# A one-core encoder layer whose mixing stage is put in another order: forward transforms before the heads, spectral products between the heads' steps, the inverse in the last head

## The chip, the cores and the metric

The kernel runs on one core of one Trainium2 chip. The metric is the device time of one execution in microseconds; lower is better.

## What is computed

One layer of an encoder trunk on a sequence of 512 tokens of width 1024, all in float32:

```
x = x + 0.5 * swiglu(rmsnorm(x), w_gate, w_up, w_down)        # first half-step, d_ff 2816
p = rmsnorm(x) @ w_in           # -> q | k | v | x0 | x1 | v_hy, each 512 wide
a = differential attention      # 4 heads, two softmaxes per head (64 wide each), T5 bias:
                                #   attn = p[:, 0] - lam * p[:, 1]; out = rmsnorm(attn @ v)
y = hyena(x0, x1, v_hy)         # width-3 conv on each; v = v_hy * x1;
                                # v = irfft(rfft(v, 1024) * rfft(kern, 1024)) + v * bias;
                                # y = rmsnorm(v * x0) in 8 groups of 64
x = x + concat([a, y]) @ w_out
x = x + 0.5 * swiglu(rmsnorm(x), ...)                         # second half-step
out = rmsnorm(x)
```

The filter `kern` comes out of a small network with sines, times a decay.

## The kernel before, in words

Five engines run programs written out by hand, one block each (SyncE, GpSimd, ScalarE, VectorE, TensorE; SP, POOL, ACT, DVE and PE below), tied together by semaphores alone; no scheduler moves anything. Activations lie transposed in SBUF, 128 channels by 512 tokens to a block `k`.

**Weight tiles.** All dense products run in float32 split into two parts. A weight tile of 8 blocks of 128x128 is loaded by SP into one of four `raw` buffers (512 KB), ACT rounds it into `w_hi` (`split`, L447), DVE makes `w_lo = raw - w_hi` (`split`, L713), each into one of two halves, and PE runs 24 matmuls per tile, `w_hi*hi`, `w_hi*lo`, `w_lo*hi` for each of 8 blocks (`tile`, L1137 to L1139). A load waits for the split of the tile four before, a split for PE to have used the tile two before. Everything else is woven into this stream.

**Stages.** First half-step (44 gate and up tiles, 24 down tiles), mixing, second half-step, final norm. The mixing stage has 24 projection tiles (`project`, matmuls of 8 blocks of x with one 128-wide part of `w_in`) and 8 output tiles (`out_half`). The token norm is applied after the product: `sum_squares` (L1150) sums over channels with one 128x128 matmul of ones on 512 columns, ACT takes the root and DVE the reciprocal (L753) of all 512 columns in `rinv`.

**A head** before the change has 6 projections (q, k, v, x0, x1, v_hy of head and group h). Between them stand four blocks of `scores` (L1255 to L1257, 2 banks of 128x512 for one block of 128 queries). Their way on: DVE `logits` (scale and bias, L904, then the row's extreme, L909), ACT `exps` (L557), DVE `combine` (L914 to L919), which normalises both softmaxes and writes `attn`. `attend` (L1278, L1286) turns `attn` on PE, ACT copies it (L577), PE multiplies it by v. `attend(h)` comes in the next head, behind its second projection. The three hyena projections get their width-3 conv by ACT `tap` and DVE `taps` (L926, L927).

**After the last head** come, in this order on PE: the kernel's forward transform (`kernel_sums`, L1369), column sums of squares for the attention norm (`col_sums`, L1328), `attend(3)`, the spreading of the inverse norms over a bank (`spread`, L1356), the forward transform of the signal (`forward`, L1403), output tile 0, then `inverse(0)` (L1417), output tile 1, the rest of the inverse, output tile 2 around the hyena's column sums (L1332) and spreads, output tiles 3 to 7. The transforms are split by parity of tokens and by near and far half of the spectrum (f = 0, 1). The spectral product per f is 4 sums of even and odd parts (L1050 to L1057), 8 products (L1041), the real parts (L1077 to L1086) on DVE, and the imaginary parts on POOL (L413 to L430).

```
combine(near, prod[:, 4, :], prod[:, 5, :], ALU.add)        # POOL, L417
mult(prod[:, 0, :], near_a, near_p)                         # DVE, L1041
nc.vector.tensor_tensor(near_a, prod[:, 0, :], prod[:, 1, :], ALU.subtract)   # L1077
pe.wait_ge((spec_set, spec_q_set)[k], f + 1)                # PE, ahead of inverse(f)
```

## Time and profile before

| what | value |
| --- | --- |
| device time, median of 3 runs | 1061.95 us (1061.38 to 1062.06) |
| device time of the profiled execution | 1061.0 us |
| its span, first to last instruction | 1059.2 us |
| mean granted TensorE clock | 0.99 |
| PE, DVE, ACT, POOL busy | 98%, 54%, 32%, 6% |
| mixing stage on PE (first projection to last output tile) | 378.4 to 685.1 us |
| DMA | 96.69 MB, mean 91 GB/s |

The profiled execution took 1061.0 us on the clock that the runs are timed with, of which 1059.2 lie between its first and last instruction. A PE that is busy 98% of the span has a matmul in flight almost always; it does not say that the matmul ran at the full clock, which is told by the granted clock (1.00 is 2.4 GHz, 0.50 is 1.2 GHz). A fp32 matmul that is not split (`L1369`, `L1403`, `L1286` and others) appears as two records in the trace, a transpose and a split matmul as one.

### The profile page before, as it was taken

To read this page: it belongs to the slowest core of one execution; us is meant where nothing else is said; L and a number is where in the kernel's file an instruction comes from. 1 tells how busy PE (TensorE), PEld (TensorE's weight loads), DVE (VectorE), ACT (ScalarE), POOL (GpSimd) and SP (SyncE) were. 2 spreads that over 40 slices of the span, in tenths; PEclk is the share of its full clock that TensorE was granted. 3 is DMA by queue.
4 is the path that set the end of the run, shared out by engine and by line. 5 is a ranking of instruction groups with operands and counts; after the bars stand their busy time and mean duration, and the time that the engine had idled before them with its cause. 6 is when DMAs were issued, how large, how long until landed. Compare 5 with 4: busy or idle time off the path is not lost. (4 is left out here: it accounts for less than half of the span.)

```text
span 1059.2 us, 12002 instructions
## 1 busy us (share of the span) xinstructions
PE 1034.5 (98%) x4551; PEld 821.8 (78%) x4551; DVE 569.8 (54%) x722; ACT 335.2 (32%) x477; POOL 60.7 (6%) x57
## 2 busy tenths in 40 slices
PE   9999999999999999999999969999999999999996
PEld 8887888888777867777775558878888888888885
DVE  5545444454544458695876695764544444433332
ACT  6222222222222333444444203532222222222222
POOL 0000000000000010000000160300000000000000
PEclk9999999999999999999999989999999999999999
DMA  7743332333233361322211000323333333333322
GB/s 221 165 118 90 100 99 86 98 95 101 83 94 105 90 199 40 97 78 80 80 60 40 1 20 21 99 87 98 94 99 99 99 99 90 96 97 91 94 70 79
DMA packets 184460, 96.69 MB, mean 91 GB/s; under 512 B 14811, under 2 KB 181859, under 8 KB 184424
## 3 DMA queue, kind: packets, MB, share of 16 engines
q1 hardware_dynamic: 183160, 92.70, 30.2%
q0 software_dynamic: 352, 1.85, 0.6%
q10 hardware_dynamic: 912, 1.64, 0.5%
q8 instruction: 24, 0.39, 0.2%
q14 instruction: 12, 0.10, 0.0%
HBM read 94.07 MB, written 2.11 MB: 91 GB/s over the span
## 5 line engine op out<-in xcount | busy, mean ns | idle before, releaser
L1137 PE MATMUL bank<-x_hi,w_hi 128*128 128x512 f32 x880 | 347.0, 394 | 0.8 <-DVE x_lo L748 0.4
L1139 PE MATMUL bank<-x_hi,w_lo 128*128 128x512 f32 x880 | 342.6, 389 | 0.0
L1138 PE MATMUL bank<-x_lo,w_hi 128*128 128x512 f32 x880 | 342.6, 389 | 0.0
L713 DVE TENSOR_TENSOR w_lo<-raw,w_hi 128x1024 fp32r<-128x1024 f32 x168 | 203.6, 1212 | 220.9 <-ACT w_hi L447 216.5
L447 ACT CAST w_hi<-raw 128x1024 fp32r<-128x1024 f32 x168 | 172.3, 1026 | 167.4 <-PE bank L1139 131.8
L1137 PEld LDWEIGHTS bank<-x_hi,w_hi 128*128 128x128 f32 x880 | 165.2, 188 | 43.2 <-issue 7.0
L1139 PEld LDWEIGHTS bank<-x_hi,w_lo 128*128 128x128 f32 x880 | 165.2, 188 | 34.7
L1138 PEld LDWEIGHTS bank<-x_lo,w_hi 128*128 128x128 f32 x880 | 165.3, 188 | 34.6 <-issue 1.2
L1137 PE MATMUL bank<-h_hi,w_hi 128*128 128x512 f32 x352 | 137.3, 390 | 0.0
L1139 PE MATMUL bank<-h_hi,w_lo 128*128 128x512 f32 x352 | 137.0, 389 | 0.0
L1138 PE MATMUL bank<-h_lo,w_hi 128*128 128x512 f32 x352 | 136.9, 389 | 0.0
L492 ACT CAST h_hi<-bank 128x512 f32 (+1 forms) x44 | 25.8, 587 | 199.2 <-DVE bank L808 199.2
L1137 PEld LDWEIGHTS bank<-h_hi,w_hi 128*128 128x128 f32 x352 | 66.1, 188 | 15.9 <-DVE resid L728 1.6
L1139 PEld LDWEIGHTS bank<-h_hi,w_lo 128*128 128x128 f32 x352 | 66.1, 188 | 13.8
L1138 PEld LDWEIGHTS bank<-h_lo,w_hi 128*128 128x128 f32 x352 | 66.1, 188 | 13.7
L803 DVE TENSOR_TENSOR bank<-bank,rinv 128x512 f32<-128x512 f32 x44 | 30.8, 699 | 75.4 <-PE bank L1139 75.4
L387 POOL TENSOR_TENSOR ssq<-ssq,sq 128x512 f32<-128x512 f32 x24 | 32.3, 1348 | 655.0 <-ACT sq L454 654.7
L488 ACT ACTIVATE silu<-bank 128x512 f32<-128x512 f32 x44 | 26.3, 598 | 134.4 <-DVE bank L799 134.4
L799 DVE TENSOR_TENSOR bank<-bank,rinv 128x512 f32<-128x512 f32 x44 | 30.8, 699 | 41.3 <-PE bank L1139 41.3
L811 DVE TENSOR_TENSOR h_lo<-bank,h_hi 128x512 f32 (+1 forms) x44 | 30.5, 692 | 36.7 <-ACT h_hi L492 36.7
L454 ACT ACTIVATE sq<-resid 128x512 f32<-128x512 f32 x24 | 15.1, 630 | 76.3 <-DVE resid L728 65.1
L808 DVE TENSOR_TENSOR bank<-bank,silu 128x512 f32<-128x512 f32 x44 | 30.8, 700 | 4.5
(207 smaller groups left out, 783.3 us busy)
## 6 DMA issues: line engine op xcount, KB each, us to landing
raw<-in_ffn_w_gate SPq DMA_DIRECT2D x44, 512.0 KB, 3.8
raw<-in_ffn_w_up SPq DMA_DIRECT2D x44, 512.0 KB, 3.7
raw<-in_ffn_w_down SPq DMA_DIRECT2D x32, 512.0 KB, 3.5
raw<-in_w_in SPq DMA_DIRECT2D x24, 512.0 KB, 3.7
raw<-in_ffn_w_down SPq DMA_DIRECT2D x16, 384.0 KB, 3.0
raw<-in_w_out SPq DMA_DIRECT2D x8, 512.0 KB, 3.4
x_nat<-in_x SPq DMA_DIRECT2D x4, 512.0 KB, 7.1
out<-o_nat SPq DMA_DIRECT2D x8, 256.0 KB, 2.9
```

The source lines that it names most:

```text
L387: nc.gpsimd.tensor_tensor(ssq[:], ssq[:], sq[:, b, :], ALU.add).then_inc(ssq_added, 1)
L447: nc.scalar.copy(w_hi[:, half, 0:kb, :], raw[:, slot, 0:kb, :]).then_inc(w_hi_made, 1)
L488: nc.scalar.activation(silu[:, b, :], bank[b][:], ACT.Silu).then_inc(gate_act, 1)
L492: nc.scalar.copy(h_hi[:, number(b, 2, i), :], bank[2 + b][:]).then_inc(h_hi_made, 1)
L713: nc.vector.tensor_tensor(w_lo[:, half, 0:kb, :], raw[:, slot, 0:kb, :], w_hi[:, half, 0:kb, :].bitcast(F32), ALU.subtract).then_inc(w_spl ...
L799: nc.vector.tensor_tensor(bank[b][:], bank[b][:], rinv[:], ALU.mult).then_inc(gate_scaled, 1)
L803: nc.vector.tensor_tensor(bank[2 + b][:], bank[2 + b][:], rinv[:], ALU.mult).then_inc(up_scaled, 1)
L808: nc.vector.tensor_tensor(bank[2 + b][:], bank[2 + b][:], silu[:, b, :], ALU.mult).then_inc(h_made, 1)
L811: nc.vector.tensor_tensor(h_lo[:, at, :], bank[2 + b][:], h_hi[:, at, :].bitcast(F32), ALU.subtract).then_inc(h_split, 1)
L1137: nc.tensor.matmul(dst, w_hi[:, half, k, :], hi, start=first and k == 0, stop=False)
L1138: nc.tensor.matmul(dst, w_hi[:, half, k, :], lo, start=False, stop=False)
L1139: ins = nc.tensor.matmul(dst, w_lo[:, half, k, :], hi, start=False, stop=last and k == kb - 1)
```

## The change

- **Order of projections.** `SEQ` puts the 8 projections of x1 and v_hy ahead of the heads; a head then has 4 (q, k, v, x0), `project(n)` counts them 0 to 23.
- **Transforms.** The kernel's transform is done between projections 4 and 7, the signal's forward transform at the first head (`forward(0)` before it, `forward(1)` in it). The inverse, now by group of channels (`inverse(g)`), is in head 3.
- **Spectral products** are cut into pairs of DVE operations (`cosines`, `sines`, `cross_near`, `own_far`, `real` and so on) and put between the attention steps of heads 0 to 2. POOL has no part in them any more.
- **Logits** and row extreme are one instruction (`tensor_tensor_reduce`, two rows in the order below); the bias table is multiplied by 8 where it is made. `combine` no longer scales both softmaxes: `attn = p0 - (lam * s0 / s1) * p1`, the factor 1/s0 goes into the norm's statistics afterwards. One [128, 512] multiplication by a scalar (L916) a block goes.
- **attend**: its first two turns stand inside the head's last projection tile, 3 matmuls before its end, and the rest right behind it, in the same head.
- **Token norm**: four matmuls on one column each, root and reciprocal of [128, 4], then four 128x128 matmuls that spread it (`spread_tokens`) inside the next tile, and a copy. This is also so in the second half-step.
- **Room**: the kernel's spectra lie where `resid` was. `resid` (2 MB) is stored to DRAM by SP behind the load of projection tile 3 and brought back behind the load of output tile 1, once the inverse is done.
- **Output tiles**: the hyena's half first, then the attention's. The norm of the hyena part is done around the last projection, that of the attention part between output tiles.

```diff
+OUT_TILES = [(1, 0), (1, 1), (1, 2), (1, 3), (0, 0), (0, 1), (0, 2), (0, 3)]
+OUT_BANKS = [(0, 1), (2, 3), (4, 5), (6, 7)]
+SEQ = [(4, 0), (5, 0), (4, 1), (5, 1), (4, 2), (5, 2), (4, 3), (5, 3)]
+SEQ += [(m, h) for h in range(HEADS) for m in (0, 1, 2, 3)]
...
+FORWARD_BANKS = (4, 5, 6, 7)
+INV_BANKS = (4, 5, 4, 5)
+SPREAD_BANKS = (2, 3, 2, 3)
+ATT_BANKS = (6, 7, 6, 7)
...
+    for n, (m, g) in enumerate(SEQ):
+        load(w[:, :, m * D_ATT + g * P:m * D_ATT + (g + 1) * P], KD, N_MIX + n)
+        if n == 3:
+            sp.wait_ge(resid_set, KD)
+            sp.dma_start(resid_dram, resid[:]).then_inc(resid_saved, 16)
...
+        if n == 1:
+            sp.wait_ge(resid_saved, 16)
+            sp.wait_ge(long_sum, NG)
+            sp.dma_start(resid[:], resid_dram).then_inc(resid_back, 16)
...
-        pool.wait_ge(prod_set, 2 * f + 1)
-        if f == 0:
...
-        combine(near, prod[:, 4, :], prod[:, 5, :], ALU.add)
-        ins = combine(far, prod[:, 6, :], prod[:, 7, :], ALU.add)
-        ins.then_inc(prod_read, 1)
-        pool.wait_ge(prod_read, 2 * f + 1)
...
+        nc.scalar.activation(x_r[:, 4:8], bank[7][:, 0:NT], ACT.Sqrt, bias=eps[:], scale=1.0 / D).then_inc(root_made, 1)
...
+        nc.vector.reciprocal(x_r[:, 8:12], x_r[:, 4:8]).then_inc(tok_inv, 1)
+    def widen_rinv(s):
+        dve.wait_ge(tok_spread, s)
+        nc.vector.tensor_copy(rinv[:], bank[7][:]).then_inc(rinv_made, 1)
...
-            nc.vector.scalar_tensor_tensor(logit[:, c, :], bank[2 + c][:], -(DK ** -0.5), near,
-                                           ALU.mult, ALU.subtract).then_inc(logit_set, 1)
-        for c in range(2):
-            n = 2 * (NT * h + qb) + c
-            dve.wait_ge(logit_set, n + 1)
-            nc.vector.tensor_reduce(soft[:, c:c + 1], logit[:, c, :], AX.X, ALU.min).then_inc(max_set, 1)
+            nc.vector.tensor_tensor_reduce(logit[:, c, :], bank[2 + c][:], near, -(DK ** -0.5), LEAST,
+                                           ALU.add, ALU.min, stat[:, c:c + 1]).then_inc(logit_set, 1)
...
-        dve.wait_ge(prob_set, 2 * (NT * h + qb) + 2)
-        link(nc.vector.reciprocal(soft[:, 4:6], soft[:, 2:4]))
-        link(nc.vector.tensor_tensor(soft[:, 6:7], soft[:, 5:6], lam[:, 5:6], ALU.mult))
-        link(nc.vector.tensor_scalar(prob[:, 1, :], prob[:, 1, :], soft[:, 6:7], None, ALU.mult))
+        i = NT * h + qb
+        dve.wait_ge(prob_set, 2 * i + 2)
+        s0, s1 = (stat[:, 16 + 2 * i + c:17 + 2 * i + c] for c in range(2))
+        link(nc.vector.reciprocal(stat[:, 2:3], s1))
+        link(nc.vector.scalar_tensor_tensor(stat[:, 3:4], s0, lam[:, 5:6], stat[:, 2:3], ALU.mult, ALU.mult))
         if h and qb == 0:
             dve.wait_ge(attn_turned, NT * h)
-        nc.vector.scalar_tensor_tensor(attn[:, qb, :], prob[:, 0, :], soft[:, 4:5], prob[:, 1, :],
+        nc.vector.scalar_tensor_tensor(attn[:, qb, :], prob[:, 1, :], stat[:, 3:4], prob[:, 0, :],
                                        ALU.mult, ALU.add).then_inc(attn_set, 1)
-    def taps(h, m):
-        dst = x0c[:, h, :] if m == 0 else conv[:, m - 1, :]
-        dve.wait_ge(tap_set, 3 * h + m + 1)
...
+    def cross_near(f):
+        near_a, far_a, near_b, far_b = parts(f)
+        mult(t0, near_a, kern_q[:, f, :])
+        link(mult(t1, near_b, kern_p[:, f, :]))
...
+    minus_lambda()
+    logits(0, 0)
+    first_row()
+    combine(0, 0)
+    project(10)
+    split(8, N_MIX + 12)
+    cross_near(0)
+    cross_far(0)
+    cosines(1)
+    sines(1)
+    logits(0, 1)
+    own_near(0)
+    combine(0, 1)
+    project(11)
+    logits(0, 2)
+    split(8, N_MIX + 13)
+    taps(11)
+    combine(0, 2)
+    own_far(0)
+    logits(0, 3)
+    project(12)
+    imaginary(0)
+    combine(0, 3)
+    split(8, N_MIX + 14)
+    project(13)
+    split_qk(1, 0)
+    split_qk(1, 1)
+    real(0)
+    split(8, N_MIX + 15)
+    logits(1, 0)
+    real_parities(0)
+    combine(1, 0)
+    imaginary_parities(0)
+    project(14)
+    logits(1, 1)
...
+    logits(3, 1)
+    split(8, N_OUT)
+    combine(3, 1)
+    long_read_out(0)
+    gate_long(0)
+    long_read_out(1)
+    gate_long(1)
+    logits(3, 2)
+    combine(3, 2)
+    att_means(2)
+    long_read_out(2)
+    gate_long(2)
+    logits(3, 3)
+    long_read_out(3)
+    combine(3, 3)
+    hy_inverse(0)
+    project(23)
+    hy_scale(0)
...
-        nc.tensor.matmul(bank[7][:], ones[:], ssq[:], start=True, stop=True).then_inc(ssq_summed, 1)
+        for t in range(NT):
+            ins = nc.tensor.matmul(bank[7][:, t:t + 1], ssq[:, t * P:(t + 1) * P], ones[:, 0:1], start=True, stop=True)
+        ins.then_inc(ssq_summed, 1)
+    def spread_tokens(s):
+        pe.wait_ge(tok_inv, s)
+        for t in range(NT):
+            ins = nc.tensor.matmul(bank[7][:, t * P:(t + 1) * P], x_r[:, 8 + t:9 + t].to_broadcast([P, P]), ident[:],
+                                   start=True, stop=True)
+        ins.then_inc(tok_spread, 1)
...
+    def inverse(g):
+        pe.wait_ge(spec_set, 2)
+        pe.wait_ge(attn_t_set, NT * 3)
+        wait(pe, long_read, g - 1)
+        for f in range(2):
+            for k, (spec, table) in enumerate(((kern_q, cos_i), (kern_p, sin_i))):
                 for parity in range(2):
+                    ins = nc.tensor.matmul(bank[INV_BANKS[g]][:, parity * FQ:(parity + 1) * FQ],
+                                           spec[:, f + 2 * parity, g * P:(g + 1) * P],
                                            table[:, f, parity * FQ:(parity + 1) * FQ],
                                            start=(f, k, parity) == (0, 0, 0), stop=(f, k, parity) == (1, 1, 1))
+        ins.then_inc(long_sum, 1)
...
+    project(9)
+    forward(0)
+    pe.wait_ge(qk_split, 2)
+    scores(0, 0)
+    project(10)
+    forward(1)
+    scores(0, 1)
+    project(11)
+    scores(0, 2)
+    turn_v(0)
+    project(12)
+    scores(0, 3)
+    project(13, between=lambda: attend_turns(0), at=6)
+    attend(0)
+    pe.wait_ge(qk_split, 4)
+    scores(1, 0)
+    project(14)
+    scores(1, 1)
...
+    scores(3, 0)
+    project(22)
+    inverse(0)
+    scores(3, 1)
+    turn_v(3)
+    inverse(1)
+    scores(3, 2)
+    att_sums(2)
+    inverse(2)
+    inverse(3)
+    scores(3, 3)
+    for g in range(3):
+        hy_sums(g)
+    project(23, between=lambda: attend_turns(3), at=6)
+    spread(0)
+    spread(1)
+    attend(3)
+    hy_sums(3)
+    spread(2)
+    first_out(between=lambda: spread(3))
+    for h in range(3):
+        att_spreads(h)
+    out_tile(1)
+    att_sums(3)
+    out_tile(2)
+    att_spreads(3)
+    for n in range(3, KD):
+        out_tile(n)
+    pe.wait_ge(resid_set, KD + 4)
```

The order on DVE. Before, the products of f = 0, behind the forward transform:

```order
L1062 COPY sig<-bank 1x512
L1041 TENSOR_TENSOR prod<-sig,kern_q 128x512
L1041 TENSOR_TENSOR prod<-sig,kern_p 128x512
L1041 TENSOR_TENSOR prod<-sig,kern_q 128x512
L1041 TENSOR_TENSOR prod<-sig,kern_p 128x512 x2
L1041 TENSOR_TENSOR prod<-sig,kern_q 128x512
L1041 TENSOR_TENSOR prod<-sig,kern_p 128x512
L1041 TENSOR_TENSOR prod<-sig,kern_q 128x512
L1077 TENSOR_TENSOR sig<-prod 128x512
L1078 TENSOR_TENSOR sig<-prod 128x512
L1082 COPY sig<-prod 1x512
L1083 COPY sig<-prod 1x512
```

Now a piece of head 1 (`stat` holds row statistics, `L978` is the logits with their row's extreme, `L1099` to `L1109` end the spectral product of f = 0):

```order
L1099 TENSOR_TENSOR kern_q<-kern_p 128x512
L1100 TENSOR_TENSOR kern_q<-kern_p 128x512
L986 RECIPROCAL stat<-stat 128x1
L987 SCALAR_TENSOR_TENSOR stat<-stat,lam 128x1
L990 SCALAR_TENSOR_TENSOR attn<-prob,stat 128x512
L1104 TENSOR_TENSOR kern_p<-prod 128x512
L1105 TENSOR_TENSOR kern_p<-prod 128x512
L1108 TENSOR_TENSOR kern_p<-sig_108 1x512
L1109 COPY kern_p<-x0c 1x512
L939 TENSOR_TENSOR v_t<-bank,rinv 128x512
L978 ISA logit,stat<-bank,bias 128x512
L978 ISA stat 128x1
```

The products of one f stood in one row on DVE, with the real parts behind them. Now one pair at a time stands between logits, combine and projections.

The order on PE around the inverse. Before, output tile 1 stands between its halves (`ma_hi`, `ma_lo` are the attention's normed output):

```order
L1439 MATMUL bank6<-ma_hi_122,w_hi_53 128x512
L1440 MATMUL bank6<-ma_lo_123,w_hi_53 128x512
L1441 MATMUL bank6<-ma_hi_122,w_lo_54 128x512
L1417 MATMUL bank0<-cos_i_71,spec_p_105 128x256 x2
L1417 MATMUL bank1<-cos_i_71,spec_p_105 128x256 x2
L1417 MATMUL bank4<-cos_i_71,spec_p_105 128x256 x2
L1417 MATMUL bank5<-cos_i_71,spec_p_105 128x256 x2
L1439 MATMUL bank2<-ma_hi_122,w_hi_53 128x512
L1440 MATMUL bank2<-ma_lo_123,w_hi_53 128x512
L1441 MATMUL bank2<-ma_hi_122,w_lo_54 128x512
```

Now in head 3, behind projection 22, with the numbers of the banks:

```order
L1355 MATMUL bank0<-x_hi_50,w_lo_54 128x512
L1606 MATMUL bank4<-cos_i_71,kern_q_107 128x256 x2
L1606 MATMUL bank4<-sin_i_72,kern_p_106 128x256 x2
L1606 MATMUL bank4<-cos_i_71,kern_q_107 128x256 x2
L1606 MATMUL bank4<-sin_i_72,kern_p_106 128x256 x2
L1481 MATMUL bank2<-k_hi_68,q_hi_94 128x512
L1482 MATMUL bank2<-k_lo_96,q_hi_94 128x512
L1483 MATMUL bank2<-k_hi_68,q_lo_95 128x512
L1481 MATMUL bank3<-k_hi_68,q_hi_94 128x512
L1482 MATMUL bank3<-k_lo_96,q_hi_94 128x512
L1483 MATMUL bank3<-k_hi_68,q_lo_95 128x512
L1532 MATMUL bank7<-ident_55,v_t_85 128x128 x4
```

The inverse moved from behind the heads to between the scores of the last one; what stood in front of it before was `forward` and one output tile, now it is two heads and more.

## Rows read from the trace of the kernel before

**Rows 1.** the page: busy time and share of the span of each engine
```profile
PE 1034.5 (98%) x4551; PEld 821.8 (78%) x4551; DVE 569.8 (54%) x722; ACT 335.2 (32%) x477; POOL 60.7 (6%) x57
```

**Rows 2.** windows view, the mixing stage in four stretches, columns in the first row
```profile
core 0: us, PE busy (x) PEld busy (x) DVE busy (x) ACT busy (x) POOL busy (x), PEclk, DMA share, GB/s
378.40:559.20 180.80, 177.81 (x791) 129.99 (x789) 138.26 (x220) 76.87 (x131) 4.78 (x6) 1.00 0.30 91
559.20:610.90 51.70, 50.48 (x186) 28.29 (x184) 32.98 (x50) 17.74 (x31) 5.46 (x4) 0.97 0.04 15
610.90:619.70 8.80, 0.10 (x1) 0.00 (x0) 8.71 (x6) 1.05 (x1) 8.66 (x7) 0.69 0.00 0
619.70:685.10 65.40, 64.51 (x297) 53.60 (x298) 46.19 (x53) 21.09 (x31) 16.36 (x12) 0.94 0.16 49
```

**Rows 3.** who waited for whom, TensorE alone: us in total, times, longest
```profile
PE bank L1417 <- DVE spec_p L1086: 9.3, 2, 8.8
PE bank L1286 <- ACT attn_t L577: 1.4, 4, 0.4
```

**Rows 4.** timeline of DVE over the spectral products: start us, us, operation
```profile
603.91 0.69 DVE L1041 TENSOR_TENSOR prod<-sig,kern_q 128x512 f32<-128x512 f32 x1
...
607.43 1.77 DVE L1041 TENSOR_TENSOR prod<-sig,kern_p 128x512 f32<-128x512 f32 x1
```

**Rows 5.** timeline of TensorE after the last head (xN counts records)
```profile
567.49 3.12 PE L1328 MATMUL bank<-ones,squares 128*128 128x1 f32 x24 [0.57 <-ACT squares L613]
...
583.54 3.60 PE L1369 MATMUL bank<-hdiff,sin_t 128*128 128x512 f32 x8
...
589.76 1.05 PE L1328 MATMUL bank<-ones,squares 128*128 128x1 f32 x8
...
619.77 6.05 PE L1417 MATMUL bank<-cos_i,spec_p 128*128 128x256 f32 x16 [8.76 <-DVE spec_p L1086]
...
631.14 3.61 PE L1417 MATMUL bank<-sin_i,spec_q 128*128 128x256 f32 x16
...
645.03 3.73 PE L1332 MATMUL bank<-halves,squares_h 128*128 128x2 f32 x32
```

**Rows 6.** timeline of TensorE, first matmuls of a projection behind a scores block
```profile
413.28 0.50 PE L1137 MATMUL bank<-x_hi,w_hi 128*128 128x512 f32 x1
413.62 0.40 PE L1138 MATMUL bank<-x_lo,w_hi 128*128 128x512 f32 x1
413.85 0.39 PE L1139 MATMUL bank<-x_hi,w_lo 128*128 128x512 f32 x1
```

**Rows 7.** groups of DVE by form: count, busy us, mean ns of one
```profile
L713 DVE TENSOR_TENSOR w_lo<-raw,w_hi 128x1024 fp32r<-128x1024 f32 x152 | 188.3, 1239 | 187.9 <-ACT w_hi L447 183.5 <-POOL zpad L395 0.8
...
L904 DVE SCALAR_TENSOR_TENSOR logit<-bank,bias 128x512 f32<-128x512 f32 x32 | 20.6, 686 | 8.4 <-PE bank L1257 8.2
...
L909 DVE TENSOR_REDUCE soft<-logit 128x1 f32<-128x512 f32 x32 | 20.3, 677 | 0.0
...
L919 DVE SCALAR_TENSOR_TENSOR attn<-prob,soft 128x512 f32<-128x512 f32 x16 | 12.0, 752 | 0.6
...
L916 DVE TENSOR_SCALAR prob<-prob,soft 128x512 f32<-128x512 f32 x16 | 7.8, 486 | 0.6
...
L753 DVE RECIPROCAL rinv<-rinv 128x512 f32<-128x512 f32 x2 | 6.7, 3350 | 1.6 <-ACT rinv L462 1.6
...
L852 DVE CUSTOM_DVE_ANT_0 lam_in<-lam_in 128x64 f32<-128x64 f32 x2 | 0.3, 206 | 0.0
...
L852 DVE DVE_READ_ACCUMULATOR2_ANT lam<- 128x1 f32 x2 | 0.1, 71 | 0.0
```

**Rows 8.** windows view, one whole head (head 1), columns as in Rows 2
```profile
449.60:493.80 44.20, 43.78 (x201) 32.63 (x200) 32.59 (x53) 19.42 (x34) 0.54 (x1) 1.00 0.28 82
```

**Rows 9.** DMA view of 370 to 400 us, rate in its 40 slices, and one issue
```profile
GB/s 339 164 38 257 340 64 0 0 0 0 63 258 329 68 145 382 399 369 361 352 227 156 284 328 351 313 272 87 25 229 326 185 248 331 64 0 0 0 0 0
...
raw<-in_w_in SPq DMA_DIRECT2D x5, 512.0 KB, 3.7
```

More of the change, by code:

```diff
@@ new lines, in _ @@
+            root(1)
+            for n in range(8):
+                split(8, N_MIX + n + 2)
+                tap(n)
+                for k in ((), (), (), (), (0, 1), (2,), (3,), ())[n]:
+                    kernel_even(k)
+            split(8, N_MIX + 10)
+            qk_high(0, 0)
+            for g in range(NG):
+                turned_values(g)
+            split(8, N_MIX + 11)
+            qk_high(0, 1)
+            forward_even(0)
+            act.wait_ge(lam_dot, 2)
+            nc.scalar.activation(lam[:, 2:4], lam[:, 0:2], ACT.Exp).then_inc(lam_exp, 1)
@@ new lines, in _ @@
+            real_parities(0)
[3 more added lines that the diff above has]
+            logits(1, 1)
+            split(8, N_MIX + 16)
+            combine(1, 1)
+            cross_near(1)
+            project(15)
+            logits(1, 2)
+            split(8, N_MIX + 17)
+            combine(1, 2)
+            taps(15)
+            cross_far(1)
+            att_means(0)
+            logits(1, 3)
+            project(16)
+            own_near(1)
+            combine(1, 3)
@@ new lines, in _ @@
+            split(8, N_MIX + 18)
+            project(17)
+            split_qk(2, 0)
+            split_qk(2, 1)
+            own_far(1)
+            split(8, N_MIX + 19)
+            logits(2, 0)
+            imaginary(1)
+            combine(2, 0)
+            real(1)
+            project(18)
+            logits(2, 1)
+            split(8, N_MIX + 20)
+            combine(2, 1)
+            real_parities(1)
+            project(19)
+            logits(2, 2)
+            split(8, N_MIX + 21)
@@ L1128, in _, with tile @@
         def _(pe):
-            def tile(dst, operand, n0, stride=0, i=0, first=True, last=True, ready=None, between=None):
+            def tile(dst, operand, n0, stride=0, i=0, first=True, last=True, ready=None, between=None, at=KD // 2):
                 half = n0 % SPLIT
@@ L1167, in gate_up @@
                         sum_squares(2 * ffn)
-                    tile(bank[2 + b][:], x_ops, n + 1, 4, i)
+                    tile(bank[2 + b][:], x_ops, n + 1, 4, i,
+                         between=(lambda: spread_tokens(2 * ffn)) if first and b == 0 else None)
             def down(s, i, first=False, mlps=False):
@@ new lines, in spread @@
+            def spread(g):
+                pe.wait_ge(hy_wide, g + 1)
+                if g < 2:
+                    pe.wait_ge(logit_set, 2 * NT * HEADS)
+                else:
+                    pe.wait_ge(hy_scaled, g - 1)
+                for t in range(NT):
+                    ins = nc.tensor.matmul(bank[SPREAD_BANKS[g]][:, t * P:(t + 1) * P], squares_h[:, g, t * P:(t + 1) * P], ident[:],
+                                           start=True, stop=True)
+                ins.then_inc(hy_spread, 1)
```

1007 lines of the change are left out of this document (536 added, 471 removed).

## The prediction

> **What bounds the kernel now.** I read the page first: PE is busy 98% of the span, DVE 54% [rows 1]. So the time is PE's, and only three things can change it: work that PE has to do, time in which it stands, and time in which it runs at the lower clock. 2% of the span standing is about 20 us, and the next question is where. The windows view over the mixing stage [rows 2] answers: the stage takes 306.7 us (378.4 to 685.1) and PE is idle in it for 180.8-177.8 = 3.0, 51.7-50.5 = 1.2, 8.8-0.1 = 8.7 and 65.4-64.5 = 0.9 us, 13.8 us in all. The reader is to see that the 181 us with the heads are nearly full and that the loss sits behind them. The waits of PE [rows 3] name it: 9.3 us for `spec_p` of DVE, the real parts of the spectral product, 8.8 of them in one wait.
>
> The clock is the second loss. In the stretch before the stall the granted clock is 0.97, behind it 0.94 [rows 2]. 1.00 is 2.4 GHz and the lower level is 1.2 GHz, so a mean of 0.97 over 51.7 us costs 0.03 x 51.7 = 1.6 us of PE work, and 0.94 over 65.4 us costs 3.9 us. The timeline [rows 5] shows one place: 16 records of 256 columns took 6.05 us right behind the 8.76 us stall, and 3.61 us eleven microseconds later. Other falls stand behind 24 records of one column (567.49) and behind 32 of two columns (645.03), where PE was "busy" with next to nothing. Loss in the stage: 13.8 + 5.5 = 19.3 us. That is the most the change can win, if PE's work stays the same.
>
> Why is `spec_p` so late? The DVE timeline [rows 4]: a product takes 0.69 us at 603.91 and 1.77 us at 607.43, when POOL has begun on the imaginary parts. All of it stands in one row between the forward transform and the inverse, and PE has only one output tile (24 matmuls at 0.23 [rows 6], 5.5 us) to put in front.
>
> **The change part by part.**
>
> 1. *Spectral products into the heads, inverse into head 3.* The 9.3 us wait goes, if the products are done by head 3. By the order on DVE the last parts of f = 1 stand in head 2, ahead of its last logits, and the inverse behind projection 22: between them lie a projection tile, `attend(2)` and another tile, over 15 us at 24 x 0.23 a tile. So nothing is late there. POOL's part moves to DVE, where an operation costs 0.69, and no operation runs at 1.77 any longer [rows 4].
>
> 2. *What DVE has to carry in the heads.* This decides the rest. Head 1 before: 32.6 us of DVE in 44.2 us [rows 8]. The head loses two projections: two products with `rinv` (1.4), two splits (2 x 1.24 = 2.5 [rows 7]), two pairs of taps (4 x 0.75 = 3.0), one product (0.7). It loses 8 searches for the extreme (8 x 0.68 = 5.4) and 4 scalings (4 x 0.49 = 2.0) [rows 7]. That leaves 17.6. It gains 12 spectral operations and two on one partition (14 x 0.69 = 9.7 [rows 4]), two small ones (0.3), and what the fused logits cost more. PE in the new head 1 has 44.2 - 2 x 5.5 - 0.5 (turning of values) = 32.7 us. The fused instruction is in the trace at 64 elements only: 206 ns and 71 ns for the read of its accumulator [rows 7]. Lower bound: the logits as now (0.69) plus 0.07. Upper bound: the sum of the two that it replaces, 0.69 + 0.68 = 1.36. Of the 206 ns at 64 elements little can be length, and the group nearest is the scalar_tensor_tensor on the same operands, so I take 0.76: plus 0.6 for the 8. DVE then has 28.2 us in 32.7, 86%; before it was 74%. At the upper bound it is 33.0 us, just over PE. I take: DVE keeps pace.
>
> 3. *`attend` in its own head.* Its turns need the last `combine` of the head, and stand 7/8 of a tile (4.8 us) behind the last scores. The way is two logits (1.5), one projection and a pair of products that DVE does while ACT makes the exponentials (2.0), `combine` (0.16 + 0.16 + 0.75), with some 0.3 of handing over: 4.9 us. PE came a tile and a half later before. The bounds are 0 and 2 us a head; I take 0.5 a head, 2.0 us. The four waits of `attend` for ACT's copies (1.4 us) [rows 3] should go, since three matmuls stand between turn and use.
>
> 4. *Token norm.* Removed each time: one matmul of 512 columns, two records at 3.60/8 = 0.45 us, 0.9 us, and the reciprocal of 3.35 us on DVE [rows 7], which lies beside the second tile and costs nothing now. Added: 8 records of one column, which took 1.05 us at 589.76 [rows 5], and 8 for the spreading, taken alike. +1.2 us each, two times, +2.4 us. The trace shows 8 records of one column at 0.13 us a record; the Trainium skill ("TensorE: Matmul & The Clock Gate", "Wait — 56ns, not 53.3ns?") puts the floor from start to start of such a small matmul at about 25 ns and a 128-column one at 56 ns. By that page the two norms would save 0.2 us each instead of costing 1.2, and the sum below would be nearly 3 us better; the row decides, and it says five times the page's floor. In the first tiles the longer chain (root, reciprocal, matmuls, copy, projection 0, split) ends some 0.7 us behind the start of projection 2: +0.7.
>
> 5. *More changes between fp32 blocks and split matmuls.* The first split matmul behind a block of another kind takes 0.34 instead of 0.23 us to the next [rows 6], 0.11 more. I count 32 such places now and 14 before: 18 x 0.11 = +2.0 us.
>
> 6. *Norms at the end.* The hyena's norm for groups 0 to 2 is behind the scores and a tile. For group 3 the chain is projection 23, tap, taps, gate, square, column sums, root, reciprocal, widen, spread, scale, round, low part: about 13 us at 0.6 to 0.8 us a step, with 13 us of PE work beside it. I take +1.3 us; bounds 0 and 5. The 24 records of two columns (`hy_sums`) stand ahead of a tile, as those at 567.49 do now. I take one fall of the clock, 1.6 us as in that stretch.
>
> 7. *`resid` to DRAM and back.* 2 MB each. Slices of the DMA view reach 350 to 400 GB/s [rows 9], which gives 5 to 6 us; I take up to 12. Behind the store wait the loads of tiles 4 and on, needed some 25 us later; behind the return the load of output tile 2, needed over 30 us later. A load lands in 3.7 us [rows 9]. Cost nothing; if the cover were gone (return over 20 us), the excess is paid in full. SP's wait for the last residual holds nothing else.
>
> The fused logits, the smaller `combine`, the order of output tiles: their work is DVE's, counted above.
>
> **Sum.** -19.3 (all loss now) + 2.0 + 2.4 + 0.7 + 2.0 + 1.3 + 1.6 = -9.3 us. The profiled execution took 1061.0, the median of runs is 1061.95, 0.1% apart, so the difference carries over: 1052.6 us, 0.9% less.
>
> **The rivals.**
>
> *A. As above*, -6 to -15: chance 0.72. The best end is all of terms 3, 5 and 6 at nothing but the norms' 2.4 us, with little of the old idle coming back: 1046.
>
> *B. DVE becomes the bound of the heads.* At 1.36 us per fused logits the head 1 balance is 33.0 against 32.7, and with the waits for its own results (some 15 links of 0.1) 1.8 us late; heads 0 and 2 alike about 1.5 each; and each `attend` waits 1.2 more, 4.8 in four. Together +8: 1060.5, no difference. For it: 86% leaves little for hand-overs. Against: DVE stood at 74% with both instructions. Chance 0.14.
>
> *C. The clock falls at the many small blocks: slower.* PE now gets sums on one column, turns and spreads at some twenty places inside the tile stream instead of in one part behind it. If a fall of 1.6 to 2.4 us [rows 2, 5] comes with each of the blocks of narrow records (two token norms, four attention sums, hyena sums, spreads, inverse pieces), it decides from about five falls more than I counted (no gain) and at ten it gives +8: about 1070. For it: two of three falls now stand behind narrow records. Against: the 8 narrow records at 589.76 are followed by no fall, and the clock through the heads is 1.00 with transposes in every one [rows 2]. Chance 0.07.
>
> *D. The end is late*: term 6 at its upper bound and the return of `resid` or the attention norm in the way of output tiles, +5: 1057.5. Chance 0.07.
>
> **How the numbers follow.** The likeliest is A, 1052.6. The range goes from A's best, 1046, over D to B, 1060. A measurement of this kernel tells 0.2%, about 2 us, from no change. Faster by more than that: all of A and D, and half of B, 0.86. Within it: the other half, 0.07. Slower: C, 0.07.
>
> **What would show it.** PE's wait for the spectra gone from its waits, and DVE at about 80 to 90% in the windows of heads 0 and 1 with PE idle under 1 us a head. Fused logits near 0.7 us each. Mixing stage near 296 us. The granted clock 1.00 in the heads, one short stretch under it near the hyena's sums. Wrong would be: DVE without a gap through the heads and PE waiting for `attn` at each `attend` (B); low clock stretches in the heads with no wait of PE (C); a wait of PE for `raw` or `w_lo` near output tile 2 (D).

## The result and the profile after

The changed kernel takes 1045.03 us (median of 4 runs, 1043.82 to 1046.0), the kernel before 1061.69 (1061.38 to 1062.06): ratio 0.9842, 95% interval 0.9825 to 0.9859, 16.7 us faster. A second set on another chip gave 1044.89 and 0.9845 (0.9827 to 0.9863). The forecast was 1052.6, range 1046 to 1060: the direction and the place were right, the gain was put at little more than half of what it is, and the time lies 1 us below the range.

The page of the changed kernel answers to [rows 1]: DVE 32 us less, POOL 21 us less, PE 6 us less in a span that is 15.0 us shorter (1044.2 against 1059.2).

```profile
PE 1028.3 (98%) x4579; PEld 820.4 (79%) x4579; DVE 537.6 (51%) x736; ACT 333.4 (32%) x478; POOL 39.2 (4%) x43
```

The windows view, columns as in [rows 2]: the mixing stage, and in it head 1, which answers to [rows 8].

```profile
378.30:669.00 290.70, 287.42 (x1285) 210.59 (x1283) 196.00 (x339) 115.40 (x195) 13.75 (x13) 0.99 0.27 85
508.20:541.60 33.40, 32.97 (x159) 24.03 (x158) 28.93 (x59) 15.61 (x30) 1.07 (x2) 1.00 0.26 78
```

The stage lasts 290.7 us where it was 306.7, so 16.0 us went there, and 1.1 us came in the second half-step. PE stands in the stage for 3.3 us instead of 13.8. In head 1 DVE is busy 28.93 us of 33.4 (87%; the prediction said 28.2 of 32.7, 86%) and PE waits 0.4 us. What PE waits for, as in [rows 3]:

```profile
PE bank L1353 <- DVE w_lo L765: 2.7, 4, 1.2
...
PE bank L1674 <- DVE mh_lo L1137: 0.9, 1, 0.9
...
PE bank L1532 <- DVE v_t L939: 0.4, 1, 0.4
```

The spectra and ACT's copies of `attn_t` are gone from the list. What is new in the stage stands at four places: `w_lo` of the second and third tile, `v_t` once, `mh_lo` once; of the 2.7 us for `w_lo`, 0.57 lie at the start of the second half-step. The instructions whose price the prediction had to guess, among the groups of DVE by form (columns as in [rows 7]):

```profile
L978 DVE CUSTOM_DVE_ANT_0 logit<-bank,bias 128x512 f32<-128x512 f32 x32 | 20.8, 687 | 11.2 <-PE bank L1483 8.1 <-issue 1.9 <-DVE sig L1019 0.7
...
L978 DVE DVE_READ_ACCUMULATOR2_ANT stat<- 128x1 f32 x32 | 2.6, 82 | 0.0
```

0.687 + 0.082 = 0.77 us for a logit with its extreme; 0.76 was taken. And the one fall of the clock in the stage, behind the hyena's column sums, in the timeline of PE (columns as in [rows 5]):

```profile
599.23 2.84 PE L1622 MATMUL bank<-halves,squares_h 128*128 128x2 f32 x24
...
602.71 0.45 PE L1353 MATMUL bank<-x_hi,w_hi 128*128 128x512 f32 x1
602.95 0.63 PE L1354 MATMUL bank<-x_lo,w_hi 128*128 128x512 f32 x1
603.37 0.63 PE L1355 MATMUL bank<-x_hi,w_lo 128*128 128x512 f32 x1
```

From 602.95 to 606.35 the matmuls stand 0.43 us apart instead of 0.23: 3.4 us at 1.2 GHz, 1.7 us lost; 1.6 was forecast. The fall is not in every execution. The profile of the second set has the same 24 records and the clock at 1.00 behind them:

```profile
598.00:602.00 4.00, 4.00 (x33) 3.54 (x30) 2.96 (x8) 2.60 (x5) 0.00 (x0) 1.00 0.82 270
602.00:606.40 4.40, 4.40 (x22) 3.58 (x21) 0.54 (x3) 1.82 (x5) 0.00 (x0) 1.00 0.98 386
```

So the mechanism of case A stands, and what has to be explained is a sum: -9.3 us forecast, -15.0 between the two profiled executions. The forecast's own best case was close: its terms for attend, changes of kind and the end at nothing leave -19.3 + 2.4 = -16.9 us, 1045.1, and it put the end of the range at 1046. Theory: the prediction took back too much of the 19.3 us (attend, changes between kinds of matmul, norms), and a wait costs more than the idle time shows. Rival: the terms were right, and something else was won, such as an effect of DVE's smaller load.

### The profile page after: what moved, and what is told of

It reads as the page before. It is cut to its first block, busy times and chain, and to the rows that moved or that the text cites. A ratio compares the mean times of both kernels' runs of the same rounds, so it can differ in the third digit from the quotient of the medians.

```text
span 1044.2 us, 12116 instructions
## 1 busy us (share of the span) xinstructions
PE 1028.3 (98%) x4579; PEld 820.4 (79%) x4579; DVE 537.6 (51%) x736; ACT 333.4 (32%) x478; POOL 39.2 (4%) x43
## 4 chain that ended last, share of the span: by engine, by line
PE 93%; DVE 4%; ACT 1%; DMA 1%; issue 1%; ACTq 0%; SPq 0%; DVEq 0%
PE bank L1353 27%; PE bank L1355 26%; PE bank L1354 26%; PE bank L1606 1%; PE bank L1542 1%; PE bank L1507 1%; DVE w_lo L765 1%; DMA x_nat<-in_x 1%; PE bank L1659 1%; PE bank L1661 1%; PE bank L1497 1%; PE bank L1660 1%; PE bank L1566 1%; PE bank L1481 1%; PE bank L1549 1%
## 5 line engine op out<-in xcount | busy, mean ns | idle before, releaser
L1354 PEld LDWEIGHTS bank<-h_lo,w_hi 128*128 128x128 f32 x352 | 66.1, 188 | 13.6
```

The source lines that it names most:

```text
L1354: nc.tensor.matmul(dst, w_hi[:, half, k, :], lo, start=False, stop=False)
```

## The experiments

The letters x, y and z in the names stand for three sets of runs, each on one chip, with the kernel before in each set. Where a text below compares a profile with "the changed kernel", it is the first profile of it; the profile of the second set is that of z3.

**x1, one engine for the spectral products.** The kernel before, with POOL's half of the products moved to DVE. Nothing else moves.

```diff
-            combine = nc.gpsimd.tensor_tensor
-            for f in range(2):
-                pool.wait_ge(prod_set, 2 * f + 1)
...
@@ DVE, behind spec_p of each f
+                add(near, prod[:, 4, :], prod[:, 5, :])
+                ins = add(far, prod[:, 6, :], prod[:, 7, :])
...
+                minus(spec_q[:, 2 * f, :], near, far)
+                ins = add(spec_q[:, 2 * f + 1, :], near, far)
```

> Kernel before, with POOL's imaginary parts of the spectral products moved to DVE and nothing else moved. Theory (sharing): the 8.8 us stall is the price of POOL and DVE at work at once: from 605 to 620 nine DVE instructions stand 1.5 to 1.8 us apart that stand 0.61 apart alone, so spec_p(0) comes 8.4 us earlier and the first wait goes. DVE then does some 5 us of imaginary parts before f = 1, so the second wait for spec_p grows from 0.5 to about 3.5 us. Net of both and of the clock: 6 to 9 us faster, 1053 to 1056. Rival (row order, as the prediction told it): what costs is that all products stand in one row between forward transform and inverse; then POOL's share was a help, and taking it away gives no change or up to 4 us slower.

Measured: 1057.72 us, ratio 0.9955 (0.9935 to 0.9975), some 4.8 us faster by the ratio, 3.6 by the medians. The timeline of DVE has the products 0.6 us apart throughout, where [rows 4] show 1.77 us for one:

```profile
604.70 0.69 DVE L1011 TENSOR_TENSOR prod<-sig,kern_q 128x512 f32<-128x512 f32 x1
...
609.64 0.69 DVE L1048 TENSOR_TENSOR sig<-prod 128x512 f32<-128x512 f32 x1
...
612.36 0.69 DVE L1057 TENSOR_TENSOR spec_p<-sig 128x512 f32<-128x512 f32 x1
```

From the first product to the first `spec_p` it is 8.35 us (604.70 to 613.05) instead of 17.0 in the kernel before, and PE goes on at 613.10 without a wait. But a new one has come:

```profile
621.65 0.77 PE L1430 MATMUL bank<-ma_hi,w_hi 128*128 128x512 f32 x1 [4.83 <-DVE sig L1027]
```

The second output tile needs the banks of the forward transform of f = 1, and DVE reads them behind 6 us of imaginary parts. DVE now works without a gap from 601.1 to 632.9. Both readings of the stall are half right: sharing with POOL made the first wait, and with that gone DVE's row itself is the bound. The gain of 6 to 9 us was over-estimated because the bank was forgotten. About 4 of the 8.8 us were to be had without any new order. How much of the rest another small change would have won is not tested; the changed kernel won it by moving the products beside the heads.

**x2, fused logits alone,** in the kernel before: `scalar_tensor_tensor` and `tensor_reduce` become one `tensor_tensor_reduce`, and the bias is stored times 8.

```diff
-                    nc.vector.scalar_tensor_tensor(logit[:, c, :], bank[2 + c][:], -(DK ** -0.5), near,
-                                                   ALU.mult, ALU.subtract).then_inc(logit_set, 1)
...
+                    nc.vector.tensor_tensor_reduce(logit[:, c, :], bank[2 + c][:], near, -(DK ** -0.5), 3.0e38,
+                                                   ALU.add, ALU.min, soft[:, c:c + 1]).then_inc(logit_set, 1)
```

> Kernel before, with the logits and their extreme in one fused instruction, nothing else. Theory: DVE was not what PE waited for in the heads (74% busy), so no change, within 1 us of 1061.7, with DVE busy about 22 us less in all. Rival: DVE's load is part of what the change won; then 2 us or more faster.

Measured: 1058.81 us, ratio 0.9973 (0.9954 to 0.9993). Faster by 2.5 to 2.9 us, with a wide interval, so the theory misses here and the rival has a part. The windows view names the place, from the first `attend` wait of head 2 to that of head 3. First the kernel before, then this one:

```profile
528.20:576.80 48.60, 47.38 (x196) 31.09 (x197) 34.07 (x57) 22.36 (x41) 0.00 (x0) 0.96 0.17 55
```
```profile
529.00:574.60 45.60, 45.14 (x196) 30.43 (x197) 29.70 (x57) 22.56 (x41) 0.00 (x0) 1.00 0.19 59
```

DVE is through with head 3 earlier, the two waits of 0.27 and 0.57 us behind it are gone, and the fall of the clock behind the 24 records at [rows 5] as well (0.96 against 1.00), which is 1.7 of the 3.0 us. This is a part of the 19.3 us, won by another route; it is no gain on top. Whether the edit took the fall away is not shown by one profile: the changed kernel has such a fall in its first profile and not in its second. Heads 1 and 2 take the same time within 0.4 us each. Ahead of them this execution has a fall of the clock (0.66 from 396 to 406 us) that the profile of the kernel before does not have; part of it lies where PE waited 1.08 us for `k_lo` before, and the same matmul behind it starts 1.9 us later (408.66 against 406.73).

**x3, unfused logits in the changed kernel.** The reverse edit, with the extreme in an instruction of its own.

> Changed kernel, with each logit made and searched in two instructions as before (0.69 + 0.68 instead of 0.77 us, 8 times a head). DVE's work in head 1 goes from 28.9 to about 33.7 us in a window of 33.4. Theory (DVE keeps pace only through the fused instruction): PE waits for attn at each attend, heads 0 to 2 grow by 1 to 2 us each, total 3 to 7 us slower than 1045. Rival 1 (the prediction's case B had it right in price): 8 us or more slower. Rival 2 (DVE has slack even so, the chain of a step decides): under 1 us.

Measured: 1050.94 us, ratio 0.9902 (0.9867 to 0.9937), 5.9 us slower than the changed kernel. Head 0 and the waits, in the windows view and the timeline of PE:

```profile
462.00:510.90 48.90, 46.47 (x187) 29.27 (x185) 42.91 (x74) 20.79 (x38) 0.54 (x1) 1.00 0.18 53
```
```profile
503.80 1.06 PE L1553 MATMUL bank<-ident,attn 128*128 128x128 f32 x8 [2.43 <-DVE attn L994]
...
519.06 0.66 PE L1536 MATMUL bank<-ident,v_t 128*128 128x128 f32 x4 [1.61 <-DVE v_t L939]
...
539.56 1.06 PE L1553 MATMUL bank<-ident,attn 128*128 128x128 f32 x8 [1.03 <-issue]
```

PE waits for `attn` and `v_t` as in case B, 5.6 us in five waits (for two of them, 1.03 and 0.19 us, the profile names no releaser). So B was a sound rival; its waits cost 5.9 us here where it had 8. With 0.6 us more for each logit the kernel is bound by DVE in its heads. It still beats the kernel before by 1%, so the fused instruction is not what makes this order possible, but it carries about a third of the gain.

**x4, the token norm of before in the changed kernel** (one matmul against ones, root and reciprocal on 128x512, in both places).

> Changed kernel with the token norm of before: one matmul against a matrix of ones, root and reciprocal on 128x512, in both places. By the prediction's terms (1.2 us each, 0.7 at the first tiles) it is 3.1 us faster than the changed kernel, 1042. By the trace of the changed kernel, where the two sums and spreads take about 0.8 us more each than the old one: 1.5 to 2.5 us faster, and the 0.66 us wait for w_lo at the third tile goes. Rival: the reciprocal of 3.35 us on DVE now stands ahead of a split that PE waits for, and the kernel is slower than 1045.

Measured: 1043.48 us, ratio 0.9819 (0.9783 to 0.9855); the times alone can't tell 1.5 us from none. In the trace the first projection tiles and the second half-step tell it. The wait at the third tile is 0.34 instead of 0.66 us; up to the turn of `v_t` in head 1 this kernel is 1.74 us ahead of the changed one, of which 0.62 us is a shorter wait at the second tile that has another cause (below), so 1.1 us is the norm's; and behind the stage it takes 373.6 us instead of 374.5, 0.95 us. The prediction had 1.2 + 1.2 + 0.7 = 3.1 us; it is 2.05. The clock fall behind the sums lasted 6.8 us in this execution instead of 3.4, which costs 1.7 us more and hides most of the gain.

**y1, the store of `resid` two loads later.**

```diff
-                if n == 3:
+                if n == 5:
                     sp.wait_ge(resid_set, KD)
```

> Changed kernel with the store of resid to DRAM two loads later (behind tile 5 instead of tile 3). Theory: the 2 MB store fills the DMA queues just when ACT issues its loads of decay (2.03 and 1.66 us to issue where before took 0.5), so ACT's w_hi for the second tile comes 2.6 us late and PE waits 1.19 us. With the store later the issues take 0.5 us again, that wait goes, and the kernel is 1.2 to 1.5 us faster than the changed one (1045.0 -> 1043.7). Rival 1: the issues are slow for another reason, no change. Rival 2: the store now lands late for kernel_spectrum(0), which must wait for it before it writes over resid; a new wait of DVE, 1 us or more slower.

Measured: 1045.17 us, ratio 0.9844 (0.9814 to 0.9873), no difference that the times can tell. The trace shows more. ACT issues three loads at the start of the stage; in the changed kernel the second and third take 2.03 and 1.66 us to issue (0.52 and 0.53 in the kernel before), and the split behind them is late:

```profile
379.23 0.43 ACTq L532 DMA_DIRECT2D decay<-in_c_decay  x1
379.69 2.03 ACTq L533 DMA_DIRECT2D decay_b<-in_c_decay  x1
...
381.75 1.66 ACTq L534 DMA_DIRECT2D w<-in_hy_f_w  x1
383.51 1.05 ACT L432 CAST w_hi<-raw 128x1024 fp32r<-128x1024 f32 x1 [3.04 <-issue]
...
385.87 0.50 PE L1353 MATMUL bank<-x_hi,w_hi 128*128 128x512 f32 x1 [1.19 <-DVE w_lo L765]
```

With the later store (timeline of the same place):

```profile
379.62 0.52 ACTq L533 DMA_DIRECT2D decay_b<-in_c_decay  x1
...
380.17 1.37 ACTq L534 DMA_DIRECT2D w<-in_hy_f_w  x1
...
381.63 1.05 ACT L432 CAST w_hi<-raw 128x1024 fp32r<-128x1024 f32 x1 [1.23 <-issue]
```

The second issue takes 0.52 us again, the third still 1.37. PE no longer waits at the second tile, and the third starts 1.4 us earlier (391.81 against 393.21). z4, which has the late store too, shows the same. But the store alone does not make the issues slow. In seven profiles with the early store (those of the changed kernel, x3, x4, y2, y3, y4) the second issue takes 1.17 to 2.06 us and PE waits 0.25 to 1.32 us; in z1 and z2, where the store starts in the same moment as ACT's first issue, it does not (z1):

```profile
386.12 0.35 SPq L363 DMA_DIRECT2D resid_dram<-resid  x1
...
386.60 0.52 ACTq L533 DMA_DIRECT2D decay_b<-in_c_decay  x1
...
387.15 1.27 ACTq L534 DMA_DIRECT2D w<-in_hy_f_w  x1
```

So the store has a part in the wait, since moving it takes the wait away in both profiles that have it later; what else must come together with it is open. The size is about 1 us in the trace; that the kernel gains it is not shown by the times.

**y2, the column sums inside tile 23,** 8 records behind each of its first three blocks of three, instead of 24 in a row ahead of it.

```diff
-            for g in range(3):
-                hy_sums(g)
-            project(23, between=lambda: attend_turns(3), at=6)
+            project(23, between=lambda: attend_turns(3), at=6,
+                    more={g: (lambda g=g: hy_sums(g)) for g in range(3)})
```

> Changed kernel with the hyena's column sums (24 narrow records in a row, ahead of tile 23) put inside tile 23, 8 behind each of its first three blocks of three. Theory: the fall of the clock behind them (3.4 us at half) goes, 1.5 to 1.7 us faster, 1043.4. Rival 1: the fall comes with narrow records wherever they stand, no change. Rival 2: the chain to the spreads starts 2 us later and PE waits for squares_h at spread(0); then no gain or up to 1 us slower.

Measured: 1044.25 us (1044.02 to 1044.67), ratio 0.9831 (0.9803 to 0.986), not to be told from the changed kernel by the times. No fall of the clock:

```profile
600.00:606.40 6.40, 6.40 (x42) 5.69 (x41) 3.00 (x10) 4.42 (x9) 0.00 (x0) 1.00 0.86 350
```

From the turn of `v_t` to the wait for `mh_lo` it takes 106.66 us, against 108.25 in the first profile of the changed kernel and 106.67 in the second, in which the clock did not fall. What the edit saves is thus the fall, 1.6 us, where it comes. How often it comes can be read from the other profiles: with the 24 records in a row ahead of tile 23 the clock falls behind them for 3.4 us in four (the first of the changed kernel, x3, y1, y4), for 6.8 us in two (x4, z1), and not at all in two (z2, z3). With the sums inside the tile it falls in neither of two (y2, z4). That fits the theory, and the narrow scatter of the four times here (0.65 us, against 2.2 for the changed kernel) does too; two profiles do not prove it.

**y3, the column sums twice,** 48 records in a row.

> Changed kernel with the same 24 narrow records done twice in a row (48). Their own time is 24 x 0.11 to 0.12 = 2.7 to 2.9 us. Theory (the fall follows from the length of the narrow stretch): the clock falls earlier, in the burst itself, and stays low longer: 4 to 5 us slower, about 1049.5. Rival (a fall is one event of fixed length, whatever the burst): own time alone, 1047.8.

Measured: 1050.96 us, ratio 0.9896 (0.9865 to 0.9927), 5.9 us slower than the changed kernel; in the trace 4.25 us over the same stretch as above. The burst and what follows:

```profile
599.46 5.92 PE L1622 MATMUL bank<-halves,squares_h 128*128 128x2 f32 x48
```
```profile
602.00:611.00 9.00, 9.00 (x41) 7.75 (x41) 1.38 (x5) 2.72 (x5) 0.00 (x0) 0.63 0.89 330
```

From its first record to the next matmul the burst takes 5.78 us instead of 2.70, and the clock is down for 6.8 us instead of 3.4; the 4.25 us of the trace lie in the theory's 4 to 5. But x4 and z1 have a fall of 6.8 us behind 24 records, so that this profile does not show that the fall grows with the length of the narrow stretch.

**y4, the first turns of `attn` behind the tile** instead of in it, in heads 0 to 2.

```diff
-            project(13, between=lambda: attend_turns(0), at=6)
+            project(13)
+            attend_turns(0)
```

> Changed kernel with the first two turns of attn behind the last tile of heads 0 to 2 instead of behind its seventh block of eight. Theory: the turns inside the tile serve only to cover ACT's copies; now PE waits for attn_t in heads 0 to 2 as before (0.3 to 0.4 us each, and some 0.15 us of drained matmul that no wait shows), 1.0 to 1.7 us slower. Rival (the prediction's term of 0.5 us a head: combine is late for the turns): the later place gives DVE 0.7 us more, and the kernel is as fast or faster.

Measured: 1048.07 us, ratio 0.9866 (0.9832 to 0.9899), 2.5 us slower; in the trace 1.57 us from the second tile to the wait for `mh_lo`. The three waits for ACT are back:

```profile
503.95 1.10 PE L1566 MATMUL bank<-attn_t,v_nat 128*128 128x512 f32 x2 [0.33 <-ACT attn_t L578]
...
537.87 1.10 PE L1566 MATMUL bank<-attn_t,v_nat 128*128 128x512 f32 x2 [0.39 <-ACT attn_t L578]
```

They show 1.10 us of idle time and cost 1.57: some 0.16 us a wait beyond the idle time. The rival, that the turns wait for `combine`, has nothing for it.

**z1 and z2, extra small blocks.** One matmul of one column (two records) in each of 28 looped tiles of the first half-step, four in each of 40 of the second; then the same with 128x128 transposes. They write to a bank that nobody reads.

```diff
+                    def extra():
+                        for _ in range((1, 4)[ffn]):
+                            nc.tensor.matmul(bank[7][:, 0:1], ident[:], ident[:, 0:1], start=True, stop=True)
```

> Changed kernel with an fp32 matmul of one column (two records each) into an unused bank in the middle of each looped gate and up tile: one in each of the 28 looped tiles of the first half-step, four in a row in each of the 40 of the second. Prediction's prices (0.13 us a record, 0.11 us for going back to split matmuls): 28 x (0.26 + 0.11) = 10.4 us and 40 x (1.05 + 0.11) = 46 us. Theory now (changes cost next to nothing, the records keep their price): 28 x 0.26 = 7.3 and 40 x 1.05 = 42. If the clock falls behind each of the groups of eight records, far more than 46 in the second.

> The same with 128x128 transposes: one in each of 28 tiles, four in a row in each of 40. From the turns of attn (four take 0.43 to 0.44 us to the next block): with 0.11 us for going back, 28 x (0.11 + 0.11) = 6.2 us and 40 x (0.44 + 0.11) = 22 us; with nothing for it 3.1 and 17.6 us. The clock stays at 1.00.

Measured, one execution each: spans 1089.5 and 1064.6 us, 45.3 and 20.4 us more than the first profile of the changed kernel. Two tiles with their block, in each stage:

```profile
117.35 0.28 PE L1392 MATMUL bank<-ident 128*128 128x1 f32 x2
117.49 0.48 PE L1353 MATMUL bank<-x_hi,w_hi 128*128 128x512 f32 x1
117.80 0.40 PE L1354 MATMUL bank<-x_lo,w_hi 128*128 128x512 f32 x1
...
123.04 0.28 PE L1392 MATMUL bank<-ident 128*128 128x1 f32 x2
```
```profile
723.14 0.95 PE L1392 MATMUL bank<-ident 128*128 128x1 f32 x8
...
729.54 0.94 PE L1392 MATMUL bank<-ident 128*128 128x1 f32 x8
```

A plain tile takes 24 x 0.2275 = 5.46 us. Here it takes 5.69 with one narrow matmul and 6.40 with four: 0.23 and 0.94, so 0.235 each and nothing for the change. With transposes it is 5.58 and 5.93: 0.12 and 0.47, again proportional. Over all tiles that makes 44 and 22 us; the spans agree with it within some 1 us, once the fall of the clock behind the hyena's sums (6.8 us in z1, none in z2, 3.4 in the changed kernel) and the missing wait at the second tile are counted. The first split matmul behind a block does take 0.31 instead of 0.23 (117.49 to 117.80), but the block ahead of it is short by as much: two narrow records take 0.14 to the next start. The clock stays at 1.00 with a group of 8 narrow records every 6.4 us (windows view, second half-step):

```profile
700.00:850.00 150.00, 150.00 (x751) 126.61 (x750) 61.69 (x71) 36.78 (x48) 0.00 (x0) 1.00 0.29 84
```

**z3 and z4, all together.** The changed kernel again, and one that has the token norm of before, the sums in tile 23, the later store, and four small moves on ACT and DVE.

> The changed kernel again, on the chip and in the rounds of the next one: 1044 to 1046 us.

> Changed kernel with what the runs so far showed: the token norm of before (2.0 us less), the hyena's sums inside tile 23 (1.6), the store of resid two loads later (1.3), one x_lo of the output tiles behind the split of the next tile (the wait of 0.57 us for w_lo at the start of the second half-step), root, reciprocal and widening of the hyena's last group ahead of other work and its spread one block earlier (most of the wait of 0.95 us for mh_lo), the product for v_t of head 1 ahead of two small operations (0.4). If the savings add up: 6 to 7 us faster than the changed kernel, 1038.5. Rival: regained idle time comes back elsewhere or as a fall of the clock, then 3 us or less.

Measured: 1044.89 (1043.77 to 1047.92) and 1040.73 us (1040.3 to 1041.26), ratios 0.9845 (0.9827 to 0.9863) and 0.9797 (0.9782 to 0.9813). 4.2 us faster than the changed kernel and 20.8 faster than the one before: it beats both, by two thirds of what was hoped. The waits of `v_t` and at the second tile are gone, that for `mh_lo` is 0.29; the third tile still waits 0.63 us for `w_lo`, where x4 alone had 0.34. Two remain at the start of the second half-step, one of them new:

```profile
664.25 0.47 PE L1349 MATMUL bank<-x_hi,w_hi 128*128 128x512 f32 x1 [0.48 <-DVE w_lo L765]
...
669.69 0.50 PE L1349 MATMUL bank<-x_hi,w_hi 128*128 128x512 f32 x1 [0.42 <-DVE x_lo L804]
```

The `x_lo` that was moved behind a split is what PE waits for next, and the split gained 0.1 us. The second half-step ends only 0.35 us sooner, where the norm alone had given 0.95.

## Why the prediction was right and wrong

- *What bounds the kernel* held: PE, and 19.3 us of standing and low clock in the mixing stage, most of it behind the heads. The 9.3 us wait for the spectra is gone, and x1 adds what the long part of it was made of. What the 19.3 us leave out is the part of each wait that the idle time does not show.
- *Step 2, DVE* held to 0.7 us in head 1 and 0.01 us for the fused instruction. x3 shows that at 1.36 us per logit the waits of case B come, at 5.9 of its 8 us.
- *Step 3, attend, +2.0*: 0. No `attend` waits. The chain was written down as 4.9 us against 4.8 of cover and then rounded up to half a microsecond a head: this term was mis-sized. And the moved turns cover ACT's copies, which with the hidden part of each wait is worth 1.6 us in three heads (y4).
- *Step 4, token norm, +3.1*: 2.05 (x4), 0.8 and 0.95 us of work where 1.2 was taken each time, and 0.3 us of wait at the third tile where 0.7 was taken. The 1.05 us of [rows 5] is how long eight records are in flight; the next matmul starts before the last of them ends, and what eight cost in a stream is 0.94 us (z1). The Trainium skill ("TensorE: Matmul & The Clock Gate", "Wait — 56ns, not 53.3ns?") has floors of about 25 and 56 ns from start to start; an estimate from them makes the two norms a saving. No record here comes near them: a one-column fp32 matmul (two records) costs 0.235 us and a 128-column transpose 0.12, so the row was right to decide.
- *Step 5, changes of kind, +2.0*: 0 by z1 and z2. This is the step that failed in kind: one interval of 0.34 us was read as the price of any change. [rows 6] stand behind a block of `scores`, and there the steps are long on both sides (the same timeline, a little wider):

```profile
412.06 0.39 PE L1139 MATMUL bank<-x_hi,w_lo 128*128 128x512 f32 x1
412.37 0.50 PE L1255 MATMUL bank<-k_hi,q_hi 64*128 64x512 f32 x2
412.71 0.40 PE L1256 MATMUL bank<-k_lo,q_hi 64*128 64x512 f32 x2
412.94 0.40 PE L1257 MATMUL bank<-k_hi,q_lo 64*128 64x512 f32 x2
413.28 0.50 PE L1137 MATMUL bank<-x_hi,w_hi 128*128 128x512 f32 x1
413.62 0.40 PE L1138 MATMUL bank<-x_lo,w_hi 128*128 128x512 f32 x1
```

  From 412.06 to 413.62 it is 0.42 us more than five steps of 0.2275. That price is paid at 16 blocks of `scores`, before and after alike. What the change added are blocks of fp32 matmuls and transposes; behind these the first interval is 0.31 us, and the block is short by as much. There were also 24 such intervals before, not 14 (counting those of 0.29 to 0.4 us in the split streams), against 32 now.
- *Step 6, end*: +1.3 forecast, 0.95 us of wait for `mh_lo`. The clock: 1.6 forecast, 1.7 in the first profile, none in the second.
- *Step 7, `resid`, 0*: 1.2 us in the first profile, 0.46 in the second, as far as the wait at the second tile is the store's (y1). I asked which loads wait behind the store on SP's queue, and not who else issues DMAs at that moment. Not forecast either: 0.43 us for `v_t`, 0.57 for a split at the start of the second half-step.
- Together, steps 3 and 5 took back 4.0 us that did not come, and step 4 took back 1.05 too much; against that stand 1.2, 0.43 and 0.57 us of waits that no term held.
- *Rival C* is refuted by z1: groups of 8 narrow records inside the tile stream cost no clock. In the first profile of the changed kernel the fall at 602.6 us is the only one in the stage. *D* did not come.

The sum by the measured terms, for the stage: -19.3 + 1.1 (norm, its first place, with its part of the third tile's wait) + 0.34 (the rest of that wait, still there in x4) + 0.95 (`mh_lo`) + 1.7 (clock) + 1.2 (second tile) + 0.43 (`v_t`) = -13.6 us, against -16.0 measured. (The 0.57 us lie behind the stage: with 0.95 for the norm and less an old wait of 0.39 they make the 1.1 us of the second half-step.) Of the 2.4 us between them the hidden part of waits takes some: 11 waits in the stage before and 4 now. It is some 0.16 us at those in y4 and at the 8.76 us stall, ahead of which stands this matmul:

```profile
610.62 0.39 PE L1441 MATMUL bank<-ma_hi,w_lo 128*128 128x512 f32 x1
```

Without a wait the next would have started 0.23 us behind it; it started 9.15 us behind it (619.77), so 8.92 us are lost and 8.76 shown. 7 x 0.16 = 1.1 us. The four waits of `attend` may hold some 0.4 us more: the 64 transposes of `attn` took 1.0 us less from start to start after the change, idle time taken out, and 4 x 0.16 of that is counted. What remains, 0.9 to 1.3 us, is open. The scatter of the kernel before is of the same size: its 20 runs beside x1 to x4 lie between 1059.65 and 1067.0 us, and the longer ones have the lower mean clock.

## What to carry to other kernels

Fill an idle stretch of the bounding engine by giving the slow engine's work to the time in which it stands beside full work; before that, see whether another engine at work beside it has made it slow, since undoing that may give a good part of the gain for a small edit (here 4.8 us, where the whole change gave 16.7). Read a price for a kind of instruction from the length of a whole repeated stretch, never from one interval: what one neighbour takes longer the other may take shorter, and a price read beside one kind of block need not hold beside another. And when a large transfer is added, look at every engine that issues a DMA in those microseconds, the compute engines' own queues too.

## What was not expected of the hardware

- DVE and POOL at once on 128x512 fp32 operands: DVE instructions 1.5 to 1.8 us apart instead of 0.61, and back to 0.6 when POOL has none (x1).
- Issuing a DMA from ACT took 2.03 and 1.66 us instead of 0.5 while a 2 MB store was under way, and ACT's next instruction began 3.04 us late; in z1 and z2 it took 0.52 and 1.2 to 1.3 us beside the same store.
- The clock fall behind 24 narrow records in a row comes in some executions and not in others of the same kernel (first profile and z3), and lasted 3.4 us in four and 6.8 us in two of the eight profiles with the same burst; groups of 8 between split matmuls brought none in 40 tiles.
- Around a block of split matmuls on 64 rows (`scores`) the step in takes 0.31 and the step out 0.34 us instead of 0.23, and so does the first step of either kind behind them (0.34). From a split matmul on 128 rows to a block of fp32 it is 0.23 us.
